# Diagonal matrices of inverse softmax sums in place of the identity, in the second and third attention of a three-layer block on one core

## The chip, the cores and the metric

The kernel runs on one core of a Trainium2 chip. The time is the device time of one execution in microseconds; the kernel before was timed in three runs, with a median of 2087.43 us and values from 2087.04 to 2091.03 us.

## The reference, cut to what matters

The program computes a stack of three blocks over 512 positions of width 1024, all in float32: a differential attention, a windowed attention with grouped keys and sinks, and a forgetting attention, each with projections and gated feed-forward parts around it. The change touches only how the softmax of the second and of the third attention is divided by its sum:

```python
# windowed attention (16 query heads, 4 key heads, blocks of 128 positions)
m = jnp.maximum(jnp.max(s, axis=-1, keepdims=True), sink)
e = jnp.exp(s - m)
pr = e / (jnp.sum(e, axis=-1, keepdims=True) + jnp.exp(sink - m))
o = jnp.einsum('bnhgqc,bnchd->bnqhgd', pr.astype(v.dtype), vb)
...
# forgetting attention (8 heads, causal, blocks of 128 queries)
p = jax.nn.softmax(s, axis=-1).astype(vh.dtype)
return jnp.einsum("bhqk,bhkd->bhqd", p, vh)
```

## The kernel before, in words

Activations are kept with the channels on the 128 partitions and the 512 positions along the row. Every large product is split: each float32 operand is written as a high and a low part in a rounded format (tiles with `hi` and `lo` in their names), and `mm3` (L546) issues three matrix products, high by high, high by low and low by high. Weights come in slabs of 128 x 1024 by DMA into `raw`; ScalarE rounds them to `whi` (L1090), GpSimd subtracts to get `wlo` (L536).

The three attentions are run by three functions of the same name, `attention(kind)`, one on TensorE, one on VectorE and one on ScalarE, each with kind 1, 2 or 3. The order is written by hand: a loop over steps `g`, four steps (one for each block of 128 queries) per pair of heads. Kind 2 has 8 pairs, so 32 steps, kind 3 has 4 pairs, so 16 steps. A step handles two heads `s`, and for its query block `nb` blocks of 128 keys: 2, 3, 3, 2 in kind 2 (the window), 1, 2, 3, 4 in kind 3 (causal). That makes 160 blocks of 128 x 128 in kind 2 and 80 in kind 3.

In step `g` each engine does, in this order:

- TensorE: `scores(g + 2)` (kind 2) or `scores(g + 1)` (kind 3); a quarter of a projection of later queries or keys as long as there are any (`piece`; in kind 2 for g up to 23, after the transposes where g is a multiple of 4), in kind 3 also parts of a gate's product from step 12 on; then `transposes(g)`, and in every second step `outputs(g - 1)`, the product with the values.
- VectorE: `maxima` of the scores just made, rotation of new queries and keys (`rope`, `q_low` L1743) or, in kind 3, their norm and some taps of a convolution (L2147), `normalise(g + 1)`, then `prob_low(g)`.
- ScalarE: the exponentials (L1207), which also give their sums, `prob_high(g)` (L1228, the transposed probabilities rounded from PSUM to `pthi`), and its share of the rest.

`normalise` adds the sink's term to the sums (kind 2, L1782), inverts the sums of both heads (L1793), and multiplies the probabilities of each head, `nb` x 128 columns, in place by the inverse sum of their row (L1797). `transposes` waits for that, and for `prob_low` of the step before, because a head's transposed probabilities stand in one of two PSUM banks (2 and 3) until `prob_low` (L1805) has read them. It then issues one transpose by TensorE for each block (L773), with the probabilities as the loaded operand and the identity as the one that streams through. The probabilities stand in the large buffer `AR`, the identity in `constR`. Elsewhere the kernel also has plain products of two float32 operands: `spread_norm` multiplies a column that is broadcast to 128 by the identity (tile `mixc` or `rcol` by `constR`), and `norm_sum` loads 128 x 128 blocks of `acc` and streams one column of ones. Both issue four products for one norm.

Of the kernel before, what the change touches and what calls it, by code (L numbers as in the profile page):

```python
# [29 lines left out]
ALU = mybir.AluOpType  # L30
# [6 lines left out]
P = 128  # L37
# [130 lines left out]
def slab_of(stage, i, j):  # L168

    s = SLAB0[stage] + j  # L170
    return s + 4 * i, s % RING, s // RAWS + (4 // RAWS) * i
# [15 lines left out]
def build(nc, xT, pT, posd, wts, par, con, lamd, outT):  # L187
    ctx = ExitStack()
    with ctx:
        def sb(name, shape, dt=F32):  # L190
            return ctx.enter_context(nc.sbuf_tensor(name, shape, dt))

        def sem(name):
            return ctx.enter_context(nc.semaphore(name))
# [15 lines left out]
        cosT = sb("cosT", [P, T])  # L210
# [16 lines left out]
        rinv = sb("rinv", [P, 8])  # L227
# [9 lines left out]
        PS = ctx.enter_context(nc.psum_tensor("PS", [P, 8, T], F32))  # L237
# [4 lines left out]
        def ar(off, n=1):  # L242
            v = AR[:, off:off + n * T]
            return v.rearrange("p (n t) -> p n t", n=n)
# [10 lines left out]
        def ccon(name, a=0, b=None):  # L255
            o, e = CCOLS[name]
            return con_sb[:, o + a:(e if b is None else o + b)]

        def f32(a):
            return a.bitcast(F32)  # L260
# [4 lines left out]
        ident = f32(identR)  # L265
# [7 lines left out]
            return ar(0, KC)[:, (m + 2) % KC, :]  # L273

        rC, rS = ar(0)[:, 0, :], ar(512)[:, 0, :]
        swap, qraw = ar(1024, 2), ar(2048, 2)
        prob = ar(3072, 4)
        OA = ar(5120, 8)
# [6 lines left out]
        def join_gate_of(m):  # L285
# [27 lines left out]
        score_done, max_ready, exp_ready, prob_ready = (  # L313
            sem("score_done"), sem("max_ready"), sem("exp_ready"), sem("prob_ready"))
# [60 lines left out]
        def band(kind, qb):  # L375


            if kind == 1:
                return 0, TB, []
            if kind == 2:  # L380
                lo, hi = max(qb - 1, 0), min(qb + 1, TB - 1)
                masks = [(qb - 1 - lo, 1)] * (qb > 0) + [(qb + 1 - lo, 2)] * (qb < TB - 1)
                return lo, hi - lo + 1, masks
            return 0, qb + 1, [(qb, 2)]
# [71 lines left out]
        def probs(kind):  # L456
            return prob3 if kind == 3 else prob
# [84 lines left out]
        def _(pe):  # L542
# [3 lines left out]
            def mm3(out, ahi, alo, bhi, blo, start, stop):  # L546
                mm(out, ahi, bhi, start, False)
                mm(out, ahi, blo, False, False)
                return mm(out, alo, bhi, False, stop)
# [5 lines left out]
            def open_tile(stage, i, j):  # L555
                bank, before = tile_of(stage, i, j)

                pe.wait_ge(tile_free[bank], before + 1)
                return PS[:, bank, :]
# [141 lines left out]
            def all_values(kind):  # L701

                stage = f"v{kind}"
                for t in range(4, 8) if kind == 1 else range(4):
                    bank, before = tile_of(stage, 0, t)
                    pe.wait_ge(tile_free[bank], before + 2)
# [54 lines left out]
            def transposes(kind, g):  # L761
                nb = band(kind, g % 4)[1]
                if g == 0 and kind == 1:
                    all_values(1)
                for s in range(HP[kind]):
                    n = PB0[kind] + HP[kind] * g + s

                    pe.wait_ge(prob_ready, n + 1)
                    if n >= 2:
                        pe.wait_ge(pt_ready, n - 1)  # L770
                    source = probs(kind)[:, 2 * (g % 2) + (1 if kind == 1 else s), :]
                    for k in range(nb):
                        last = pe.transpose(PS[:, 2 + n % 2, k * P:k * P + P],  # L773
                                            source[:, k * P:k * P + P], ident)
                    last.then_inc(trans_done, 1)

            def outputs(kind, g):
# [76 lines left out]
            def attention(kind, norm, begin):  # L854
# [10 lines left out]
                for g in range(steps):  # L865
# [13 lines left out]
                    if kind == 3:  # L879
                        for m, part in GATES.get(g, ()):  # L880
                            gate_part(m, part)
                    transposes(kind, g)
                    if kind == 3 and g == steps - 1:
                        for part in (2, 3):
# [122 lines left out]
            for k in range(KC):  # L1007
                last = mm3(PS[0:8, 6, :], wfhi[:, 8 * k:8 * k + 8], wflo[:, 8 * k:8 * k + 8],
                           hi[:, k, :], lo[:, k, :], k == 0, k == KC - 1)
# [45 lines left out]
            for q in range(4):  # L1055
                s, slot, _ = slab_of("ao3", 0, q)
                two_tiles("ao3", s, slot, 2 * q, lambda k: pthi[:, k, :], lambda k: ptlo[:, k, :])
            for what, n in JOIN:
                s, slot, _ = slab_of("gc3", 0, JOIN_SLAB[what, n])
                first = JOIN_TILE[what, n]  # L1060
                if what == "gate":
                    weights(s)
                    out = open_tile("gc3", 0, first)
                    for k in range(KC):
                        c = slice(k * P, k * P + P)
                        last = mm3(out, whi[:, slot, c], wlo[:, slot, c], hi[:, k, :], lo[:, k, :],
                                   k == 0, k == KC - 1)
# [535 lines left out]
        def _(dve):  # L1603
            own = Own(dve, dve_step)
            tt, stt, ts = dve.tensor_tensor, dve.scalar_tensor_tensor, dve.tensor_scalar
# [165 lines left out]
            def normalise(kind, g):  # L1771


                n = SC0[kind] + 2 * g
                nb = band(kind, g % 4)[1]
                pr, c, b = probs(kind), n % 4, 2 * (g % 2)

                dve.wait_ge(exp_ready, n + 2)
                if kind == 2:

                    dve.wait_ge(sink_ready, g + 1)
                    own.step(tt(rsum[:, c:c + 2], rsum[:, c:c + 2], rsum[:, 4 + c:6 + c], ALU.add))  # L1782
                    own.wait()
                if kind == 1:
                    own.step(dve.reciprocal(rinv[:, c + 1:c + 2], rsum[:, c + 1:c + 2]))
                    own.wait()
                    own.step(stt(rinv[:, c:c + 1], sum1[:, g:g + 1], lam[:, 5:6], rinv[:, c + 1:c + 2],
                                 ALU.mult, ALU.mult))
                    own.wait()
                    stt(pr[:, b + 1, :], pr[:, b + 1, :], rinv[:, c:c + 1], pr[:, b, :],  # L1790
                        ALU.mult, ALU.add).then_inc(prob_ready, 1)
                else:
                    own.step(dve.reciprocal(rinv[:, c:c + 2], rsum[:, c:c + 2]))  # L1793
                    own.wait()
                    for s in range(2):
                        v = pr[:, b + s, 0:nb * P]
                        ts(v, v, rinv[:, c + s:c + s + 1], None, ALU.mult).then_inc(prob_ready, 1)  # L1797

            def prob_low(kind, g):
                blocks = band(kind, g % 4)[1]  # L1800
# [46 lines left out]
            def attention(kind):  # L1847
# [3 lines left out]
                if kind == 3:  # L1851
                    maxima(kind, 0)
                    head_norm(2)
                    normalise(kind, 0)
                for g in range(steps):
# [16 lines left out]
                    if g + 1 < steps:  # L1872
                        normalise(kind, g + 1)
# [180 lines left out]
            for t in range(2):  # L2054
                q_low(t, 0, t)
            maxima(1, 0)
            normalise(1, 0)
            values_low("v1", (1,), T)
            rope_sin(0)
# [41 lines left out]
            for m in range(KC):  # L2101
                c = KC * NORMS.index("mix") + m
# [364 lines left out]
```

## Time and profile before

| | value |
|---|---|
| time, median of 3 runs | 2087.43 us |
| span of the profiled execution | 2087.8 us |
| TensorE busy | 2043.2 us (98%) |
| VectorE busy | 1224.2 us (59%) |
| ScalarE busy | 941.6 us (45%) |
| GpSimd busy | 904.8 us (43%) |
| mean granted TensorE clock | 0.992 |

The profile gives of the profiled execution's own time only its span, from the first to the last instruction; it stands 0.4 us above the median of the timed runs and inside their spread. A TensorE record's duration holds the time that the result needs to leave the engine, so records overlap, and the cost of one in a stream is the distance from its start to the next one's start. PE is TensorE, PEld its loads of the stationary operand, DVE is VectorE, ACT ScalarE, POOL GpSimd. A granted clock of 1.00 is 2.4 GHz, one of 0.50 is 1.2 GHz.

In the program's time the second attention lies at about 745 to 893 us, the third at about 1440 to 1547 us.

### The profile page before, as it was taken

Reading aid. Unit: us, or ns where it says so; the run is one execution under the profiler, and the core shown is the slowest. Engines: PE = TensorE matmul, PEld = TensorE weight load, DVE = VectorE, ACT = ScalarE, POOL = GpSimd, SP = SyncE. Lnnn points to the kernel's source line nnn. Section 1 sums busy time; section 2 is a strip of 40 time slices with the busy share of each in tenths; the row PEclk is TensorE's granted clock in tenths of the full one; section 3 lists DMA queues with packets and bytes.
Section 4 is the critical chain, followed back from the end, with each engine's and each line's share of the span. In section 5 each row is a group of like instructions: output and inputs, shape, how many; then the busy total and the mean of one; then the engine's idle time right before and its main releaser. Section 6 shows DMA issues by size and latency. Waiting matters only on the chain.

```text
span 2087.8 us, 28730 instructions
## 1 busy us (share of the span) xinstructions
PE 2043.2 (98%) x9976; PEld 1684.1 (81%) x9976; DVE 1224.2 (59%) x1842; ACT 941.6 (45%) x1495; POOL 904.8 (43%) x660
## 2 busy tenths in 40 slices
PE   7999999999999999899999999999999999999999
PEld 6777788888887878788888887878888788888887
DVE  6677857546265789856636266548879473213222
ACT  5456645434245567635424245535742544322222
POOL 4322235545456431044645456444215454455454
PEclk9999999999999999999999999999999999999999
DMA  4222122332323211022333223222103222232323
GB/s 169 81 76 76 48 75 98 103 101 91 101 91 121 81 61 32 31 91 81 101 101 101 92 99 112 91 81 92 39 23 107 85 91 92 90 110 92 101 91 111
DMA packets 52756, 183.21 MB, mean 88 GB/s; under 512 B 6576, under 2 KB 6832, under 8 KB 52656
## 3 DMA queue, kind: packets, MB, share of 16 engines
q1 hardware_dynamic: 51072, 177.76, 25.9%
q10 hardware_dynamic: 1584, 4.07, 0.5%
q8 instruction: 68, 1.11, 0.2%
q14 instruction: 32, 0.26, 0.0%
HBM read 176.04 MB, written 2.10 MB: 85 GB/s over the span
## 4 chain that ended last, share of the span: by engine, by line
PE 53%; issue 24%; POOL 13%; DVE 7%; ACT 2%; POOLq 0%; DVEq 0%; DMA 0%; ACTq 0%; SPq 0%
PE PS L544 52%; POOL wlo L536 13%; DVE AR L1915 1%; PE PS L773 1%; DVE AR L1918 0%; DVE acc L1630 0%; DVE ptlo L1805 0%; DVE AR L1797 0%; DVE nmax L1753 0%; ACT AR L1187 0%; DVE AR L2277 0%; ACT AR L1323 0%; DVE AR L1931 0%; DVE Blo L1935 0%; DVE Blo L2281 0%
## 5 line engine op out<-in xcount | busy, mean ns | idle before, releaser
L536 POOL TENSOR_TENSOR wlo<-raw,whi 128x512 fp32r<-128x512 f32 x656 | 904.6, 1402 | 1169.7 <-ACT whi L1090 1168.5
L544 PE MATMUL PS<-Bhi,whi 128*128 128x512 f32 x2352 | 927.7, 394 | 17.2 <-DVE Blo L1623 10.8
L544 PE MATMUL PS<-Blo,whi 128*128 128x512 f32 x2352 | 917.6, 390 | 0.0
L544 PE MATMUL PS<-Bhi,wlo 128*128 128x512 f32 x2352 | 917.4, 390 | 0.0
L1090 ACT ACTIVATE whi<-raw 128x1024 fp32r<-128x1024 f32 x328 | 345.2, 1056 | 510.7 <-PE PS L544 435.4
L544 PEld LDWEIGHTS PS<-Bhi,whi 128*128 128x128 f32 x2352 | 442.5, 188 | 123.1 <-issue 14.1
L544 PEld LDWEIGHTS PS<-Bhi,wlo 128*128 128x128 f32 x2352 | 442.6, 188 | 93.7
L544 PEld LDWEIGHTS PS<-Blo,whi 128*128 128x128 f32 x2352 | 443.0, 188 | 89.3 <-issue 0.5
L1614 DVE TENSOR_TENSOR AR<-PS,R 128x512 f32<-128x512 f32 x170 | 115.3, 690 | 235.9 <-PE PS L544 224.1
L1670 DVE TENSOR_TENSOR X<-X,PS 128x512 f32<-128x512 f32 x88 | 60.3, 687 | 227.2 <-PE PS L544 226.5
L1915 DVE SCALAR_TENSOR_TENSOR AR<-AR,par_sb 128x511 f32<-128x511 f32 x88 | 117.6, 1336 | 8.8 <-ACT AR L1323 8.8
L1338 ACT ACTIVATE Bhi<-AR 128x512 f32 x66 | 41.8, 633 | 167.7 <-DVE AR L1931 167.7
L1918 DVE SCALAR_TENSOR_TENSOR AR<-AR,par_sb 128x511 f32<-128x511 f32 x88 | 106.8, 1213 | 12.9 <-DVE AR L1915 2.9
L1207 ACT ACTIVATE AR<-PS,nmax 128x512 f32<-128x512 f32 (+3 forms) x160 | 93.2, 590 | 44.1 <-DVE nmax L1756 41.7
L1323 ACT ACTIVATE AR<-AR,par_sb 128x512 f32<-128x512 f32 x88 | 71.0, 806 | 38.5 <-DVE AR L1614 38.5
L1935 DVE TENSOR_TENSOR Blo<-AR,Bhi 128x512 f32 x66 | 47.1, 714 | 62.1 <-ACT Bhi L1338 62.1
L1623 DVE SCALAR_TENSOR_TENSOR Blo<-X,par_sb,Bhi 128x512 fp32r<-128x512 f32 x56 | 63.0, 1135 | 34.9 <-ACT Bhi L1116 27.7
L1228 ACT ACTIVATE pthi<-PS 128x512 fp32r<-128x512 f32 (+3 forms) x128 | 56.4, 477 | 59.1 <-PE PS L773 58.4
L1931 DVE TENSOR_TENSOR AR<-AR 128x512 f32<-128x512 f32 x66 | 56.1, 849 | 36.3 <-ACT AR L1334 27.2
L1630 DVE TENSOR_TENSOR acc<-acc,sq 128x512 f32<-128x512 f32 x56 | 73.2, 1308 | 0.0
L773 PE MATMUL PS<-constR,AR 128*128 128x128 f32 x368 | 58.3, 286 | 10.6 <-DVE ptlo L1805 9.7
L1805 DVE TENSOR_TENSOR ptlo<-PS,pthi 128x512 fp32r<-128x512 f32 (+3 forms) x128 | 64.3, 534 | 6.7 <-ACT pthi L1228 6.7
(237 smaller groups left out, 2069.1 us busy)
## 6 DMA issues: line engine op xcount, KB each, us to landing
raw<-in_weights SPq DMA_DIRECT2D x328, 512.0 KB, 3.2
AR<-AR SPq DMA_DIRECT2D x56, 64.0 KB, 2.0
X<-in_xT ACTq DMA_DIRECT2D x4, 512.0 KB, 6.9
out<-X SPq DMA_DIRECT2D x8, 256.0 KB, 3.0
AR<-in_pT ACTq DMA_DIRECT2D x2, 512.0 KB, 3.9
par_sb<-in_parameters ACTq DMA_DIRECT2D x1, 314.0 KB, 8.5
AR<-in_positions ACTq DMA_DIRECT2D x1, 256.0 KB, 8.3
con_sb<-in_constants ACTq DMA_DIRECT2D x1, 198.5 KB, 8.1
```

Source lines behind the costliest of these rows:

```text
L536: ins = pool.tensor_tensor(wlo[:, j, c], raw[:, j % RAWS, c], f32(whi[:, j, c]), ALU.subtract)
L544: return pe.matmul(out, w, x, start=start, stop=stop)
L773: last = pe.transpose(PS[:, 2 + n % 2, k * P:k * P + P], source[:, k * P:k * P + P], ident)
L1090: act.activation(whi[:, slot, :], raw[:, slot % RAWS, :], ACT.Copy)\
L1207: act.activation(probs(kind)[:, 2 * (g % 2) + s, 0:nb * P], PS[:, score_bank(kind, n), 0:nb * P], ACT.Exp, bias=nmax[:, n % 4:n % 4 + 1], ...
L1323: act.activation(cv[:, 2 * pair + u, :], us[:, 2 * pair + u, :], ACT.Identity, scale=conv_w[:, l, 1, u, bass.ds(q, 1)], bias=conv_w[:, l, ...
L1614: tt(out, PS[:, bank, :], R[:, :], ALU.mult).then_inc(tile_free[bank], 1)
L1623: stt(chunks(Blo[b])[:, m, :], X[:, m, :], gain(name, col, m), f32(chunks(Bhi[b])[:, m, :]), ALU.mult, ALU.subtract).then_inc(x_split, 1)
L1630: tt(acc[:, :], acc[:, :], sq[:, slot, :], ALU.add).then_inc(sq_used, 1)
L1805: tt(transposed(ptlo, kind, g, s), PS[:, 2 + n % 2, 0:blocks * P] .rearrange("p (k q) -> p k q", k=blocks), f32(transposed(pthi, kind, g, s)),
L1915: own.step(stt(c[:, 1:T], x[:, 0:T - 1], conv_w[:, l, 0, u, bass.ds(q, 1)], c[:, 1:T], ALU.mult, ALU.add))
L1918: stt(c[:, 0:T - 1], x[:, 1:T], conv_w[:, l, 2, u, bass.ds(q, 1)], c[:, 0:T - 1], ALU.mult, ALU.add).then_inc(conv_done, 1)
```

## The change

VectorE no longer multiplies the probabilities. For each head it multiplies the identity (the float32 copy in `con_sb`) by the inverse sums, which gives a 128 x 128 diagonal matrix, whatever `nb` is. There are four such matrices, in the columns of `cosT`, a tile of 512 columns that nothing else uses in these stretches. TensorE then multiplies each block of probabilities by the diagonal matrix of its head where it transposed it by the identity before: the result is the transposed block with its columns scaled. In place of the transpose instruction this is the plain product `mm` of two float32 operands. The first attention (kind 1) keeps the transpose. On every engine the instructions stand in the same order as before: 47 groups of transposes on TensorE and 48 pairs of multiplications on VectorE are exchanged in place (48 steps; at the end of the second attention the transposes of two steps adjoin and count as one group), and no wait or increment is added or moved.

```diff
+        diag = cosT[:, :].rearrange("p (n c) -> p n c", n=4)
...
                     for k in range(nb):
-                        last = pe.transpose(PS[:, 2 + n % 2, k * P:k * P + P],
-                                            source[:, k * P:k * P + P], ident)
+                        out, c = PS[:, 2 + n % 2, k * P:k * P + P], slice(k * P, k * P + P)
+                        if kind == 1:
+                            last = pe.transpose(out, source[:, c], ident)
+                        else:
+
+                            last = mm(out, source[:, c], diag[:, 2 * (g % 2) + s, :], True, True)
                     last.then_inc(trans_done, 1)
...
                     own.step(dve.reciprocal(rinv[:, c:c + 2], rsum[:, c:c + 2]))
                     own.wait()
                     for s in range(2):
-                        v = pr[:, b + s, 0:nb * P]
-                        ts(v, v, rinv[:, c + s:c + s + 1], None, ALU.mult).then_inc(prob_ready, 1)
+
+                        ts(diag[:, b + s, :], ccon("ident"), rinv[:, c + s:c + s + 1], None, ALU.mult)\
+                            .then_inc(prob_ready, 1)
```

## Rows read from the trace of the kernel before

**Rows 1.** The page: busy time by engine; then TensorE's busy share in 40 slices.

```profile
PE 2043.2 (98%) x9976; PEld 1684.1 (81%) x9976; DVE 1224.2 (59%) x1842; ACT 941.6 (45%) x1495; POOL 904.8 (43%) x660
...
PE   7999999999999999899999999999999999999999
```

**Rows 2.** Windows of both attentions: stretch, its length, busy time (and records) by engine.

```profile
757.00:857.00 100.00, 98.14 (x704) 81.73 (x705) 91.57 (x265) 71.16 (x209) 17.75 (x14) 0.98 0.12 38
857.00:886.00 29.00, 21.25 (x159) 18.37 (x158) 25.79 (x77) 21.86 (x64) 2.51 (x2) 0.88 0.06 19
1459.00:1505.00 46.00, 45.51 (x348) 38.41 (x347) 37.95 (x82) 31.74 (x65) 8.07 (x6) 1.00 0.11 36
1505.00:1531.00 26.00, 21.23 (x157) 18.61 (x158) 24.15 (x53) 15.60 (x38) 2.98 (x2) 0.80 0.06 22
1531.00:1548.00 17.00, 17.00 (x116) 14.73 (x115) 11.87 (x25) 6.85 (x18) 0.00 (x0) 1.00 0.00 0
```

**Rows 3.** Line 773: all its transposes; then those of the stretch 757 to 857 us.

```profile
L773 PE MATMUL PS<-constR,AR x368: 270/272/476, 89.9 to 1546.4; 128*128 128x128 f32 x184
...
757.00:857.00 100.00, 17.85 (x120) 13.99 (x120) 0.98 0.12 38
```

**Rows 4.** Timeline of TensorE, transposes in the second attention: start us, duration us, operation.

```profile
788.47 0.60 PE L773 MATMUL PS<-constR,AR 128*128 128x128 f32 x4
...
789.96 0.74 PE L773 MATMUL PS<-constR,AR 128*128 128x128 f32 x4
...
796.59 0.82 PE L773 MATMUL PS<-constR,AR 128*128 128x128 f32 x6
797.51 0.39 PE L544 MATMUL PS<-qkhi 64*128 64x256 f32 x2
```

**Rows 5.** Timeline: four products in `spread_norm`; weight loads of four in `norm_sum`.

```profile
1382.98 1.05 PE L544 MATMUL PS<-constR,mixc 128*128 128x128 f32 x8
1383.79 0.48 PE L544 MATMUL PS<-Bhi,whi 128*128 128x512 f32 x1
...
681.60 1.08 PEld L544 LDWEIGHTS PS<-con_sb,acc 128*128 128x128 f32 x8
```

**Rows 6.** Groups of VectorE instructions, shapes apart, line 1797: busy us, mean ns of one.

```profile
L1797 DVE TENSOR_SCALAR AR<-AR,rinv 128x384 f32<-128x384 f32 x40 | 15.0, 418 | 0.7
...
L1797 DVE TENSOR_SCALAR AR<-AR,rinv 128x256 f32<-128x256 f32 x40 | 14.0, 392 | 0.7
...
L1797 DVE TENSOR_SCALAR AR<-AR,rinv 128x512 f32<-128x512 f32 x8 | 3.5, 484 | 0.1
...
L1797 DVE TENSOR_SCALAR AR<-AR,rinv 128x128 f32<-128x128 f32 x8 | 1.9, 283 | 0.1
```

**Rows 7.** Waits at 757 to 857 us, then 857 to 886 us: us, times, longest.

```profile
PE PS L544 <- DVE AR L1716: 2.4, 1, 2.4
...
PE PS L773 <- DVE ptlo L1805: 5.9, 5, 2.2
...
PE PS L544 <- DVE ptlo L1805: 1.4, 1, 1.4
```

**Rows 8.** Timeline of one step late in the second attention.

```profile
870.45 0.66 PE L773 MATMUL PS<-constR,AR 128*128 128x128 f32 x4
870.55 1.02 DVE L1753 TENSOR_REDUCE nmax<-PS 128x1 f32<-128x384 f32 x2 [1.12 <-PE PS L544]
...
872.88 0.75 DVE L1805 TENSOR_TENSOR ptlo<-PS,pthi 128x256 fp32r<-128x256 f32 x2
...
873.45 0.74 PE L773 MATMUL PS<-constR,AR 128*128 128x128 f32 x4 [1.38 <-DVE ptlo L1805]
```

**Rows 9.** Windows with the granted clock at half (third number from the end).

```profile
758.80:762.20 3.40, 3.40 (x17) 2.40 (x16) 3.29 (x10) 3.11 (x9) 1.22 (x1) 0.51 0.00 0
861.20:868.10 6.90, 5.59 (x30) 5.06 (x30) 6.48 (x21) 6.02 (x19) 2.51 (x2) 0.51 0.01 2
1520.00:1530.20 10.20, 9.25 (x49) 7.94 (x48) 9.57 (x24) 5.12 (x16) 0.00 (x0) 0.50 0.01 2
```

## The prediction

> **What bounds the kernel now.** I read the page first. TensorE is busy for 98% of the span, no other engine for more than 59%, and of the 40 slices only the first and one in the middle are below 9 tenths [rows 1]. So TensorE's own stream sets the time nearly everywhere, and time added to it is added to the kernel, except where it stands idle anyway. That makes the windows over the two attentions the second view [rows 2]. From 757 to 857 us (steps 1 to 24 of the second attention) TensorE is busy for 98.14 of 100 us. In the last steps, 857 to 886 us, no projection is left to fill its stream: 21.25 of 29 us, with VectorE at 25.79. The third attention is full up to 1505 us (45.51 of 46) and after 1531 us (17.00 of 17); between, where steps 8 to 11 have neither projection nor gate, TensorE has 21.23 of 26 and VectorE 24.15. The waits give the idle time its name: in the stretch at 857 us, 5.9 + 1.4 us are for `ptlo` of VectorE, and in the full stretch 2.4 us is one single wait for VectorE's L1716, right at the start [rows 7].
>
> **Removed: the transposes.** Kinds 2 and 3 hold 160 + 80 = 240 of the 368 transposes (the other 128 are the first attention's, unchanged), and 368 blocks leave 368 records: one record for a block [rows 3]. Six of them last 0.82 us from the first start to the last end [rows 4], the last one 0.27 us [rows 3], so they start (0.82 - 0.27) / 5 = 0.110 us apart.
>
> **Added: the float32 products.** No row shows this very product, but `spread_norm` has its twin: 128 x 128 float32 loaded, 128 float32 columns streamed. Its four products leave eight records, over 1.05 us [rows 5]; less the last one's 0.27 that is 0.78 / 7 = 0.111 us from record to record, and two records for a product: 0.223 us. A broadcast operand isn't the reason for the doubling, since four dense blocks of `acc` in `norm_sum` also take eight loads [rows 5]. So a block goes from 0.110 to 0.223 us: 0.113 us more, and 240 blocks are 27.1 us if nothing hides any of it. That is the upper end; the lower is 0, if a block's product came in one record like a transpose.
>
> The Trainium skill ("FP8 and Floating Point Precision", TensorE Precision Notes) says that a true float32 product takes four passes, and "TensorE: Matmul & The Clock Gate" (Terms) that the transpose mode is four times faster for float32. By these a block would cost four times 0.110 us rather than two. The trace has two records where the page has four passes, and it agrees in direction but not in size; the sum goes by the trace, and the page's ratio is a rival below.
>
> **Changed: VectorE's multiplication.** The 96 instructions of L1797 now take 15.0 + 14.0 + 3.5 + 1.9 = 34.4 us; each becomes one of 128 columns, and the nearest row, the same form at 128 columns, has 283 ns, so 96 x 0.283 = 27.2 us [rows 6]. VectorE gets 7.2 us back: 0.27 us for a step with three blocks to a head, 0.22 with two, 0.40 with four, nothing with one. The other end is nothing saved. Where TensorE is the bound this is worth 0, because its work hides it.
>
> **What of it is on the path.**
>
> Step 0 of the second attention (4 blocks) stands before the wait of 2.4 us for L1716 [rows 7]: 0.45 us is hidden there. If this cover is gone it costs just that.
>
> Steps 1 to 24 hold 120 blocks [rows 3], all in the full stream: 120 x 0.113 = 13.6 us. Against it stand small waits that longer products cover. After a burst of six transposes the scores start 0.92 us after its first start [rows 4], though 5 x 0.110 + 0.20 (the same distance after an undisturbed burst, an estimate) would be 0.75; with 0.68 us more work ahead this 0.17 us goes, six times: 1.0 us. And every fourth step has two bursts 1.5 us apart, of which the second takes 0.74 us against 0.60 for the first [rows 4], since its banks are still being read; the longer first burst covers that: 6 x 0.14 = 0.8 us. What is left is 13.6 - 1.8 = 11.8 us.
>
> Steps 25 to 31 hold 36 blocks, 4.1 us. Of two consecutive steps, the one without `outputs` is VectorE's: after the scores at 870.4 it works without a break through maxima, inverse, multiplication and `ptlo` up to 873.6, while TensorE waits 1.38 us for it [rows 8]. There the longer product (0.45 to 0.68 us) is hidden, and VectorE's 0.22 to 0.27 us come through. In the other step TensorE runs through transposes, `outputs` and scores and waits hardly at all, so the product counts in full. I take half of each: +2.0 us, and half of VectorE's 1.7 us back, -0.8: +1.2 us. The ends are -1.7 (all hidden) and +4.1.
>
> Third attention: 80 blocks. Steps 0 to 7 and 12 to 15 are in full stretches [rows 2] and step 11 is followed by full work: 68 blocks. Of the 12 of steps 8 to 10 I count 2 as exposed, the rest stands beside VectorE's chain. 70 x 0.113 = 7.9 us; VectorE's gain in steps 9 to 11, 0.22 + 0.27 + 0.40 = 0.9 us, shortens that chain: +7.0 us. The ends are +6 and +9.
>
> The clock: inside the attentions TensorE was granted half its clock for 3.4, 6.9 and 10.2 us, the second and third of these in and behind the stretches with idle time [rows 9, 2]. Half speed costs at most half of each, 10.2 us together, less where TensorE waits anyway. The change fills some of that idle time, which speaks for shorter half-clock stretches, but the stretches also shift; I take -1.0 us, with -9 and +4 as ends.
>
> **The sum.** 11.8 + 1.2 + 7.0 - 1.0 = 19.0 us. The profiled span of 2087.8 us becomes 2106.8; since it lies 0.4 us above the median of the runs, I predict 2106.5 us, 0.9% slower.
>
> **The rivals.**
> - *The half clock goes.* If the idle time that goes takes all three half-clock stretches with it, up to 9 us come back instead of 1: 2098.5 us. For it: the two longest stand where TensorE idles most. Against: the one at 758.8 us follows a wait that stays, and half the tail's idle stays. 9%.
> - *Everything exposed, and new waits behind it.* `pthi` and with it `ptlo` come up to 0.68 us later in a step; if VectorE and ScalarE have no slack for that, the tail's steps grow too: 27.1 us and some for further waits, about 2117 us. Against: VectorE reaches `ptlo` long after `pthi` is there [rows 8]. 7%.
> - *VectorE is the bound (the other side).* If `ptlo`, not TensorE's stream, set the pace of all steps of both attentions, the products would run in idle time and the 7.2 us of VectorE would be the result: 2080.5 us. It decides from the point where TensorE's idle time in these stretches exceeds the 27.1 us added; the five stretches have 1.86 + 7.75 + 0.49 + 4.77 + 0 = 14.9 us [rows 2], half of it in two short ones. 2%.
> - *No doubling.* If a dense block by a diagonal matrix left one record like a transpose, only VectorE's gain in the short stretches would count: about 2086 us. Both rows of float32 products speak against it. 2%.
> - *Four times.* If a block went to 4 x 0.110 us, 0.33 us more, 240 blocks would add 79 us, less some 8 hidden: about 2159 us. Against it the same rows. 1%.
>
> **How the numbers follow.** The forecast has 79%, between 2100 and 2114 us. The range for 8 times in 10 reaches a little into the two nearest rivals: 2099 to 2115 us. A measurement of this kernel can tell about 0.2% (4 us) from no change. Faster by more than that: the VectorE rival and a sliver of others, 0.03. Within it: no doubling, 0.02. Slower: 0.95.
>
> **What the profile after should show.** 480 records for 240 blocks, at 0.11 us from start to start, under line 546 with `cosT` and `AR`; 128 transposes left. The 96 multiplications at about 283 ns each. The stretch of steps 1 to 24 some 12 us longer with TensorE still full; the late steps' waits for `ptlo` shorter; the rest of the program unchanged to within a microsecond or two. One record for a block, or records at another distance, would break the main term; an attention that grows by less than 15 us together with full half-clock stretches would mean that more is hidden than I took.

## The result and the profile after

The changed kernel takes 2101.41 us (median of six runs, 2099.98 to 2105.55) against 2087.31 for the kernel before in the same comparison: 14.1 us more, ratio 1.0068 with a 95% interval from 1.0057 to 1.0079. Forecast were 2106.5 us and +19.0 us. On another chip, measured again beside the experiments, the ratio was 1.0068 (1.0055 to 1.0082).

The profiled span went from 2087.8 to 2099.7 us. The page after, first busy times, then TensorE's busy share in 40 slices, as in [rows 1]:

```profile
PE 2061.4 (98%) x10216; PEld 1709.3 (81%) x10216; DVE 1223.0 (58%) x1842; ACT 945.3 (45%) x1495; POOL 903.2 (43%) x660
...
PE   7999999999999999999999999999999999999999
```

TensorE has 240 records more and 18.2 us more busy time; every other engine is within 4 us of before. The one slice in the middle that was below 9 tenths, over the late steps of the second attention, shows a 9 now.

The products, by tile, and VectorE's part, as groups (busy us, mean ns of one, idle time before), as in [rows 3, 6]:

```profile
L546 PE MATMUL PS<-cosT,AR x480: 270/275/551, 752.1 to 1558.3; 128*128 128x128 f32 x160
```

```profile
L1803 DVE TENSOR_SCALAR cosT<-con_sb,rinv 128x128 f32<-128x128 f32 x96 | 24.8, 301 | 1.7
```

480 records for 240 blocks: two for each, where a transpose left one. The 96 multiplications keep VectorE busy for 24.8 us where L1797 took 34.4; I had put them at 27.2. One of them lasts 301 ns, a little more than the 283 I took; the busy time is less than 96 times that because instructions overlap in it.

Timeline of TensorE, the same places as in [rows 4], start and duration in us:

```profile
788.31 1.05 PE L546 MATMUL PS<-cosT,AR 128*128 128x128 f32 x8
...
797.06 1.50 PE L546 MATMUL PS<-cosT,AR 128*128 128x128 f32 x12
798.49 0.39 PE L546 MATMUL PS<-qkhi 64*128 64x256 f32 x2
```

Twelve records of six blocks last 1.50 us; less the last one's 0.27 that is 1.23 / 11 = 0.112 us each, so 0.224 us a block. The forecast had 0.223. The scores start 1.43 us after the burst does; it was 0.92.

The windows at the places of [rows 2], shifted with the program:

```profile
760.20:864.60 104.40, 104.40 (x801) 92.71 (x800) 88.80 (x251) 68.27 (x195) 15.39 (x13) 1.00 0.11 36
864.60:893.00 28.40, 23.25 (x204) 21.56 (x203) 25.32 (x78) 21.79 (x64) 2.52 (x2) 1.00 0.07 20
1465.00:1514.00 49.00, 49.00 (x375) 42.48 (x375) 37.51 (x84) 32.82 (x66) 8.07 (x6) 1.00 0.11 39
1514.00:1541.00 27.00, 22.89 (x196) 20.84 (x193) 22.39 (x50) 15.81 (x38) 2.98 (x2) 0.94 0.06 20
```

In the late steps TensorE still idles, but its granted clock, the third number from the end, is 1.00 there instead of 0.88. In steps 8 to 11 of the third attention it is 0.94 instead of 0.80.

To see where the time went, the start of the same burst of blocks is read from each kernel's timeline, and the program cut at five places: A from step 0 to step 25 of the second attention, B from there to step 0 of the third, C to its step 8, D to its step 12, E to the end. The last two columns are the us at half clock inside B and D; a piece at half clock that begins up to 0.5 us before B is counted whole. Each row comes from one profiled execution. The rows of the experiments are used below.

| kernel | A | B | C | D | E | half B | half D |
|---|---|---|---|---|---|---|---|
| before | 106.7 | 597.7 | 47.6 | 24.8 | 556.0 | 6.8 | 10.2 |
| changed | 116.9 | 596.9 | 51.4 | 24.2 | 558.2 | 0 | 3.4 |
| changed, again | 117.0 | 597.0 | 51.4 | 22.9 | 558.2 | 0 | 3.4 |
| product by the identity | 117.4 | 597.7 | 51.4 | 24.9 | 558.2 | 0 | 3.4 |
| diagonal not used | 106.9 | 598.9 | 47.1 | 22.9 | 555.9 | 10.2 | 6.8 |
| product twice | 141.4 | 603.3 | 60.3 | 24.7 | 562.7 | 0 | 0 |
| rounded product, kind 2 | 105.3 | 605.0 | 51.4 | 22.7 | 558.2 | 27.3 | 0 |
| second attention alone | 117.0 | 596.7 | 47.5 | 24.9 | 555.9 | 0 | 10.2 |
| third attention alone | 106.7 | 597.5 | 51.4 | 22.9 | 558.2 | 6.8 | 3.4 |
| product in late steps only | 106.4 | 596.9 | 47.5 | 24.1 | 556.0 | 0 | 3.4 |
| late transposes twice | 106.7 | 597.7 | 47.5 | 25.0 | 555.9 | 3.4 | 10.2 |
| product in full steps only | 116.6 | 600.0 | 51.4 | 24.7 | 558.2 | 10.2 | 10.2 |
| rounded in full steps | 105.2 | 597.2 | 47.5 | 24.2 | 556.0 | 3.4 | 3.4 |

From step 0 on the changed kernel is 10.2 - 0.8 + 3.8 - 0.5 + 2.2 = 14.9 us longer, within a microsecond of the medians' 14.1. The two spans differ by only 11.9 because the changed kernel reached step 0 at 752.1 us and the profile of before at 755.1. That isn't the change's: the same changed kernel, profiled again, reached it at 755.2 us, and the kernel with the change in the second attention alone, whose code up to there is the same, at 755.7 us. The first attention waits for the small transfers of `exchange`, and these waits differ between executions:

```profile
DVE AR L1743 <- DMA AR<-AR: 5.6, 9, 1.2
```

```profile
DVE AR L1743 <- DMA AR<-AR: 9.9, 10, 2.1
```

The first is the wait in the changed kernel from 85 to 265 us (us, times, longest), the second the same in the kernel with the second attention alone.

### The profile page after: what moved, and what is told of

The parts are those of the page before. It is cut to its first block, busy times and chain, and to the rows that moved or that the text cites. A ratio compares the mean times of both kernels' runs of the same rounds, so it can differ in the third digit from the quotient of the medians.

```text
span 2099.7 us, 29210 instructions
## 1 busy us (share of the span) xinstructions
PE 2061.4 (98%) x10216; PEld 1709.3 (81%) x10216; DVE 1223.0 (58%) x1842; ACT 945.3 (45%) x1495; POOL 903.2 (43%) x660
## 4 chain that ended last, share of the span: by engine, by line
PE 55%; issue 23%; POOL 13%; DVE 6%; ACT 1%; POOLq 0%; DVEq 0%; DMA 0%; ACTq 0%; SPq 0%
PE PS L546 55%; POOL wlo L538 13%; DVE AR L1922 1%; DVE AR L1925 0%; DVE acc L1636 0%; DVE AR L2284 0%; ACT AR L1329 0%; DVE AR L1938 0%; DVE Blo L1942 0%; DVE Blo L2288 0%; ACT Bhi L1122 0%; DVE AR L1620 0%; ACT whi L1096 0%; ACT Bhi L1344 0%; DVE X L1676 0%
## 5 line engine op out<-in xcount | busy, mean ns | idle before, releaser
L546 PEld LDWEIGHTS PS<-Bhi,whi 128*128 128x128 f32 x2352 | 442.2, 188 | 120.9 <-issue 11.6
L1676 DVE TENSOR_TENSOR X<-X,PS 128x512 f32<-128x512 f32 x88 | 60.3, 687 | 227.1 <-PE PS L546 226.4
L1942 DVE TENSOR_TENSOR Blo<-AR,Bhi 128x512 f32 x66 | 47.1, 714 | 62.1 <-ACT Bhi L1344 62.1
L1938 DVE TENSOR_TENSOR AR<-AR 128x512 f32<-128x512 f32 x66 | 56.1, 849 | 36.3 <-ACT AR L1340 27.2
L1812 DVE TENSOR_TENSOR ptlo<-PS,pthi 128x512 fp32r<-128x512 f32 (+3 forms) x128 | 65.9, 535 | 13.7 <-ACT pthi L1234 12.9
L546 PE MATMUL PS<-cosT,AR 128*128 128x128 f32 x480 | 65.2, 284 | 7.0 <-DVE ptlo L1812 7.0
```

What stands on the lines that cost most here:

```text
L546: return pe.matmul(out, w, x, start=start, stop=stop)
L1676: tt(X[:, m, :], X[:, m, :], PS[:, bank, :], ALU.add)\
L1812: tt(transposed(ptlo, kind, g, s), PS[:, 2 + n % 2, 0:blocks * P] .rearrange("p (k q) -> p k q", k=blocks), f32(transposed(pthi, kind, g, s)),
```

## The experiments

Each ratio is to the kernel before on the same chip, with its 95% interval.

**Product by the identity.** VectorE scales the probabilities as before, TensorE multiplies by the identity.

```diff
-                        last = pe.transpose(PS[:, 2 + n % 2, k * P:k * P + P],
-                                            source[:, k * P:k * P + P], ident)
+                        out, c = PS[:, 2 + n % 2, k * P:k * P + P], slice(k * P, k * P + P)
+                        if kind == 1:
+                            last = pe.transpose(out, source[:, c], ident)
+                        else:
+                            last = mm(out, source[:, c], ident, True, True)
```

> The kernel before, with the transposes of the second and third attention as float32 products by the identity; VectorE scales the probabilities as before. Theory A (the doubling of the records is the whole cost, VectorE's shorter multiplication is worth only a little where VectorE sets the pace): 2102 to 2104 us, 0.5 to 2.5 us above the changed kernel's 2101.4; steps 1 to 24 of the second attention some 11 us longer than before, as in the changed kernel. Theory B (the products cost nearly their full 27 us and VectorE's 7 us were what brought it down to 14): 2108 us or more. Half-clock stretches: if the fuller stream of products is what shortened them, they are short here too (mean clock 0.996); if they shift by chance, anything from 0.992 to 0.997.

Measured: 2103.90 us, ratio 1.0074 (1.0060 to 1.0088). The whole cost of the change is there without the diagonal matrices. Its profile is 2.0 us longer than the changed kernel's; burst by burst it falls behind by 0.2 us in steps 1 to 24, 1.1 us in the late steps and 0.7 us in stretch D, so VectorE's shorter work is worth 2 us and not 7. That rests on one profile of each; the ratios of the timed runs, 1.0074 and 1.0068, overlap in their intervals. Theory A holds.

**Diagonal not used.** VectorE as changed, TensorE as before.

```diff
-                            last = mm(out, source[:, c], diag[:, 2 * (g % 2) + s, :], True, True)
+                            last = pe.transpose(out, source[:, c], ident)
```

> The changed kernel's VectorE work (diagonal matrices instead of scaled probabilities) with the old transposes by the identity; the division by the sums is thereby left out of the second and third attention. Theory A: only the short stretches in which VectorE sets the pace gain, 1 to 2.5 us: 2085 to 2086.5 us, and the half clock late in the second attention stays. Theory B: most of VectorE's 7.2 us show: 2080 to 2082 us.

Measured: 2086.43 us, 2.5 us below its before, ratio 0.9989 (0.9980 to 0.9998). From the other side about the same 2 us. The late steps kept their half clock (10.2 us of it) and stretch B is 1.2 us longer than before, although VectorE has less to do: what it saves there is taken by the clock. The two pieces of B that are longer than before, step 26 and the part from step 31 on, are pieces with time at half clock.

**Product twice.**

```diff
+                            mm(out, source[:, c], diag[:, 2 * (g % 2) + s, :], True, True)
                             last = mm(out, source[:, c], diag[:, 2 * (g % 2) + s, :], True, True)
```

> The changed kernel with each product by a diagonal matrix issued twice into the same place (four records for a block). Theory A (0.111 us a record, and the small waits were already covered by the first doubling, so the second is exposed in full in steps 1 to 24 and 3/4 of it elsewhere): 120 x 0.223 = 26.8 us in steps 1 to 24, about 20 us in the rest: 2146 to 2150 us. Theory C (the stretches have slack that a product of any length goes on using, as half of the first doubling did): 120 x 0.223 / 2 and the like, 2125 to 2130 us.

Measured: 2148.90 us, ratio 1.0290 (1.0274 to 1.0306), as theory A had it. Six blocks in the timeline are now 24 records:

```profile
807.25 2.84 PE L546 MATMUL PS<-cosT,AR 128*128 128x128 f32 x24
```

(2.84 - 0.27) / 23 = 0.112 us a record. Step 8 to step 24 of the second attention, 80 blocks, take 66.25 us before, 73.46 changed, 91.34 here. The second doubling costs 17.88 us, 0.2235 a block, in full; the first cost 7.21 us, where 80 x 0.113 is 9.04. So in these 16 steps 1.8 us of small waits were covered by the first doubling and none was left for the second. In stretch C it is 8.9 us for 40 blocks, again 0.223 each. The Trainium skill ("FP8 and Floating Point Precision", TensorE Precision Notes) gives a float32 product four passes; the trace has two records of 0.112 us for it and four only when it is issued twice, so the estimate of twice a transpose was right for this burst of 128 columns. It doesn't speak against four passes as such. With 512 columns, in the kernel before, four float32 products leave eight records too:

```profile
L544 PE MATMUL PS<-AR,con_sb x8: 591/592/592, 1617.4 to 1620.4; 128*128 128x512 f32 x8
```

(1620.4 - 1617.4) / 7 = 0.43 us a record, 0.86 us a product, where the rounded products of 512 columns just before start 0.23 us apart. There a float32 product costs close to four rounded ones.

**Rounded product in the second attention.**

```diff
+        prob2 = Bhi[1][:, 2048:4096].rearrange("p (n t) -> p n t", n=4)
+        diag2 = Blo[1][:, 2048:2560].rearrange("p (n c) -> p n c", n=4)
...
-            return prob3 if kind == 3 else prob
+            return {1: prob, 2: prob2, 3: prob3}[kind]
```

> The changed kernel, but in the second attention the exponentials and the diagonal matrices are written in the rounded format (in halves of the value buffers that are free there), so that the product is one of rounded operands; the low part of these probabilities is lost. Third attention as changed. Theory A (a record of rounded operands with 128 columns takes 0.06 us, as the value product's 128-column records do at best, and there is one for a block): steps 1 to 24 are 120 x (0.223 - 0.06) = 19.6 us shorter than changed, less some 2 us of waits that come back; total 2084 to 2088 us. Theory D (the load of 128 columns sets the distance, 0.11 us): 120 x 0.11 = 13.5 us shorter, less the same waits: 2090 to 2093 us.

Measured: 2097.74 us, ratio 1.0040 (1.0025 to 1.0055), outside both expectations. Six blocks are six records:

```profile
794.32 0.78 PE L548 MATMUL PS<-Blo,Bhi 128*128 128x128 f32 x6
```

With a last record of 0.28 us that is 0.50 / 5 = 0.10 us a block: one record instead of two, and nearly as long as a transpose, not 0.06. On the record theory A is wrong and D right, and stretch A did shrink by 11.6 us, to 1.4 us below before, as D had it (13.5 less some 2). The gain was lost in the late steps (36 us from step 25 on; third number from the end the clock):

```profile
858.40:894.40 36.00, 31.20 (x160) 28.85 (x161) 23.05 (x69) 18.54 (x55) 2.51 (x2) 0.62 0.05 16
```

The clock was at half for 27.3 us of stretch B, which is 8.1 us longer than in the changed kernel. All of that lies in the pieces with time at half clock: step 26 takes 7.08 us instead of 4.57, step 28 5.10 instead of 3.89, step 30 5.26 instead of 3.52, the part from step 31 on 2.6 us more; the steps between them are as long as in the changed kernel to 0.01 us. For the load of 128 columns "TensorE: Matmul & The Clock Gate" of the Trainium skill (LDWEIGHTS) gives columns / 1.2 in ns, by which an estimate for 128 columns is 107 ns; the distances of 0.10 to 0.112 us of all three kinds of record agree with a stream of such small products being paced by their loads, though no run separates load and stream.

**One attention alone.** The condition on `kind` is the edit.

```diff
-                        if kind == 1:
+                        if kind != 2:
                             last = pe.transpose(out, source[:, c], ident)
```

> The change made in the second attention alone; the third keeps its transposes and scaled probabilities. Theory A (each attention pays for its own blocks: about 10 us in steps 0 to 24, near nothing or a gain in the late steps, where the products stand beside VectorE's work and the half clock goes): the stretch from step 0 to the third attention grows by 9 to 10 us, as in the changed kernel, and the time is 2096 to 2099 us. By the terms of the prediction it would be 11.8 + 1.2 us, 2100 to 2101 us.

Measured: 2095.89 us, ratio 1.0033 (1.0021 to 1.0044), 7.0 us above its before and just below the expected 2096 to 2099. A + B are 9.3 us longer in the profile, which is of the slowest of its seven executions.

> The change made in the third attention alone. Theory A: its 80 blocks cost 5 to 7 us, 2092.5 to 2094.5 us, and the half clock late in the second attention (6.9 us in the profile of before) is there again, since that attention has its idle time back. Theory C (the stretches of half clock come by chance and not with TensorE's idle time): it may be missing there.

Measured (`if kind != 3`): 2095.18 us, ratio 1.0030 (1.0019 to 1.0041), 6.3 us: inside the expected 5 to 7 us, though just above the 2092.5 to 2094.5 us, since this chip's before is 2088.9. The two add to 13.3 us, the change's 14.1 within the intervals. The late steps of the second attention, with their transposes back, had half clock again, 6.8 us.

**Product in the late steps only.**

```diff
+        def by_product(kind, g):
+            return (kind == 2 and g > 24) or (kind == 3 and 8 <= g <= 11)
...
-                        if kind == 1:
+                        if not by_product(kind, g):
...
+                        v = pr[:, b + s, 0:nb * P]
+                        out, src = (diag[:, b + s, :], ccon("ident")) if by_product(kind, g) else (v, v)
+                        ts(out, src, rinv[:, c + s:c + s + 1], None, ALU.mult).then_inc(prob_ready, 1)
```

> Diagonal matrices and products only in the steps without a projection to fill TensorE's stream (25 to 31 of the second attention, 8 to 11 of the third), transposes and scaled probabilities in all others. Theory A (there the products run in TensorE's idle time, VectorE's shorter work comes through, and the half clock goes): 1 to 3 us below before, 2085 to 2087 us by the chip's before of about 2088, and steps 1 to 24 as before. Theory B (the products cost there too): 36 + 20 blocks x 0.113 = 6.3 us above before.

Measured: 2087.00 us, 1.9 us below its before, ratio 0.9988 (0.9979 to 0.9997). The 6.3 us of TensorE's work added in these steps cost little. Against the kernel with the same VectorE work and transposes (diagonal not used) step 28 is 0.4 us longer (3.88 and 3.50), step 9 of the third attention 0.2 us (4.34 and 4.18) and its step 11, which full work follows, 1.1 us (7.23 and 6.13, with 3.4 and 3.0 us at half clock). In D the half clock didn't go wholly: 3.4 us are left. The same 36 us from step 25 on, first here, then with the same VectorE work but transposes (diagonal not used):

```profile
859.20:895.20 36.00, 32.05 (x231) 28.76 (x232) 23.20 (x70) 18.98 (x56) 2.50 (x2) 1.00 0.05 16
```

```profile
859.90:895.90 36.00, 30.45 (x186) 26.50 (x187) 22.88 (x69) 18.67 (x55) 2.52 (x2) 0.86 0.05 16
```

Clock 1.00 against 0.86, and a stretch B of 596.9 against 598.9 us: the kernel that does more is through it sooner. The difference stands in step 26 (4.56 against 5.53 us) and from step 31 on (576.0 against 577.4 us), both with 3.4 to 3.6 us at half clock in the kernel with transposes.

**Late transposes twice.**

```diff
-                        last = pe.transpose(PS[:, 2 + n % 2, k * P:k * P + P],
-                                            source[:, k * P:k * P + P], ident)
+                        for _ in range(2 if (kind == 2 and g > 24) else 1):
+                            last = pe.transpose(PS[:, 2 + n % 2, k * P:k * P + P],
+                                                source[:, k * P:k * P + P], ident)
```

> The kernel before with each transpose of steps 25 to 31 of the second attention issued twice, 36 more records of 0.11 us (4.0 us of TensorE work), VectorE's work as before. Theory A (the work goes into TensorE's idle time, and with it the granted clock stays full there): the stretch from step 25 to the projections after it is as long as before or up to 1.5 us shorter, no half clock in it, time within 0.1% of before. Theory C (the clock has nothing to do with it): the stretch is about 2 us longer and has its half clock as before.

Measured: 2088.08 us, ratio 0.9994 (0.9985 to 1.0003). 4.0 us more work, stretch B as long as before to 0.1 us, half clock down from 6.8 to 3.4 us but not gone. Theory C's 2 us are not there; theory A's "no half clock" isn't either. The mean clock of its 11 timed executions is 0.9935, between the 0.9923 of this chip's before and the 0.9955 of the product in the late steps.

```profile
860.10:896.10 36.00, 32.16 (x226) 28.54 (x227) 24.87 (x69) 18.55 (x55) 2.53 (x2) 0.95 0.05 16
```

**Product in the full steps only.** The condition of `by_product` is turned round.

```diff
+            return (kind == 2 and g <= 24) or (kind == 3 and not 8 <= g <= 11)
```

> The complement of the kernel with products in the late steps only: diagonal matrices and products in steps 0 to 24 of the second attention and 0 to 7 and 12 to 15 of the third, transposes and scaled probabilities elsewhere. Theory A (the blocks of the full steps carry the whole cost, the late ones give some back): 10.2 us in steps 0 to 24 as in the changed kernel, 6.0 us in the third attention, about 2105 us, 1 to 3 us above the changed kernel on the same chip. Theory B (late steps cost too): below the changed kernel.

Measured: 2107.09 us, ratio 1.0090 (1.0075 to 1.0105), 4.4 us above the changed kernel on the same chip, with fewer products and more than the 1 to 3 us expected. The late steps here are word for word those of before, yet stretch B is 600.0 us instead of 597.7, with 10.2 us at half clock instead of 6.8 (B and D together are 4.8 us longer here than in the changed kernel again, A 0.4 us shorter):

```profile
871.40:907.40 36.00, 30.00 (x186) 26.63 (x187) 23.67 (x69) 18.04 (x55) 2.71 (x2) 0.86 0.05 16
```

**The changed kernel again.**

> The changed kernel itself, beside the others on the same chip: 2101 to 2104 us, so that the single kernels can be compared with it without the difference between chips.

Measured: 2102.68 us, ratio 1.0068 (1.0055 to 1.0082).

**Rounded product in the full steps, float32 product in the late ones.** In the second attention up to step 24 as in the rounded kernel, in the third transposes outside steps 8 to 11. The diagonal matrices are chosen by step in the same way (left out of the cut).

```diff
+            return kind == 2 or (kind == 3 and 8 <= g <= 11)
...
+            return {1: prob, 2: prob if g > 24 else prob2, 3: prob3}[kind]
```

> Second attention: in steps 0 to 24 exponentials and diagonal matrices in the rounded format and one rounded product for a block (0.10 us), in steps 25 to 31 the float32 product; third attention: the float32 product in steps 8 to 11, transposes in the rest. The probabilities of those 25 steps lose their low part. By the stretches measured apart: steps 0 to 24 1.4 us shorter than before, the late steps 0.8 us shorter, the third attention 0.8 us shorter: about 3 us below before, 2085 to 2086.5 us. If the half clock comes back in the late steps as in the kernel with rounded products throughout the second attention, it is 3 to 6 us more.

Measured: 2084.29 us, 4.0 us below its before, ratio 0.9981 (0.9971 to 0.9991): the shortest of all, and 0.7 us below the expected 2085 to 2086.5. Stretch A is 1.5 us, B 0.4 us, D 0.6 us shorter than before. It isn't the same result at a lower price: the probabilities of 25 steps lose their low part.

## Why the prediction was right in direction and a third too high

**Right: the doubling, and where it is paid.** Two records of 0.112 us for a block instead of one of 0.110 was the term that carries the sum, and both the profile after and the doubled product confirm it. In full steps without waits it is exact: stretch E has 20 blocks and grew by 2.2 us, 20 x 0.113 = 2.3.

**Right: VectorE's saving hardly counts.** I had 1.7 us for it (0.8 and 0.9); identity against diagonal shows 2.0 us: 0.5 in A, which I had at nothing, 0.8 in B and 0.7 in D. The 7.2 us that I gave as VectorE's whole saving set busy time, in which overlapping instructions count once, against 96 times a mean. Busy time against busy time it is 34.4 - 24.8 = 9.6 us. The sum didn't use it; it used the means by step.

**Too small: the waits that longer products cover.** For steps 1 to 24 I took 1.8 us off 13.6; stretch A, with step 0, grew by 10.2 us. Step 0 cost nothing, as forecast (8.27 us before, 8.23 after, from its burst to the next one's). Read so step by step, four steps repeat through the stretch; here are steps 8 to 11, in us:

| step | blocks | before | changed | grown | by count |
|---|---|---|---|---|---|
| 8 | 4 | 6.63 | 6.80 | 0.17 | 0.45 |
| 9 | 6 | 3.13 | 3.63 | 0.50 | 0.68 |
| 10 | 6 | 5.29 | 5.99 | 0.70 | 0.68 |
| 11 | 4 | 1.50 | 1.94 | 0.44 | 0.45 |

Steps 10 and 11 pay in full. In steps like 9 the 0.17 us before the scores are covered, six times, 1.1 us together, as forecast. The term that was too small is that of steps like 8: 0.28 us each instead of 0.14. Of the 0.14 us by which "takes 0.74 us against 0.60" only 0.04 went: the burst's eight records now start over 0.88 us, where undisturbed ones would over 7 x 0.111 = 0.78. What I overlooked there is TensorE's short stop before the late projection, where the distance to the next product went from 0.31 to 0.12 us. And step 24 doesn't belong to the full stretch: there VectorE's shorter work for step 25 comes through, and the step went from 5.58 to 5.26 us (5.52 with the identity, where VectorE's work is as before), so its 4 blocks, 0.45 us, were hidden. The idle time of the weight loads shows the stops, at 757 to 857 us before and 760 to 864 after:

```profile
PEld PS L544 <- issue: 7.0, 18, 2.6
PEld PS L544 <- DVE qklo L1743: 2.0, 6, 0.4
```

```profile
PEld PS L546 <- issue: 1.8, 5, 0.4
```

The two windows aren't quite the same place: 3.2 of the 7.0 us, the longest of 2.6 among them, stand before step 1. From step 1 on it is 3.8 + 2.0 us before and 1.8 after. In stretch C, of 4.5 us by count 3.8 showed: 0.4 us was hidden in step 1, which held a wait of 0.4 us for VectorE's L2214, and 0.2 in step 7, since the burst after it no longer stops 0.22 us for `ptlo`.

**Mis-sized: the late steps and the clock.** I had +1.2 us for steps 25 to 31 and -1.0 us for the clock in both attentions together. Stretch B was 0.8 us shorter, D 0.5 us shorter where my terms gave about +0.2. A step without `outputs` does hide the product, as told. The step of [rows 8], after (the view ends inside the last burst, so it counts 5 of its 8 records):

```profile
876.86 1.16 PE L546 MATMUL PS<-cosT,AR 128*128 128x128 f32 x8
876.96 1.02 DVE L1759 TENSOR_REDUCE nmax<-PS 128x1 f32<-128x384 f32 x2 [0.39 <-PE PS L546]
...
879.17 0.75 DVE L1812 TENSOR_TENSOR ptlo<-PS,pthi 128x256 fp32r<-128x256 f32 x2
879.73 0.79 PE L546 MATMUL PS<-cosT,AR 128*128 128x128 f32 x5 [0.74 <-DVE ptlo L1812]
```

From burst to burst it is 2.87 us instead of 3.00, and the wait fell from 1.38 to 0.74 us. What was wrong is the other half, the steps with `outputs`, where I counted the product in full, 2.0 us. The kernel before and the product by the identity differ in the product alone and are both at full clock in steps 27 to 30: 3.00, 3.50, 3.04 and 3.66 us against 2.99, 3.89, 3.04 and 3.66. Only step 28 pays, 0.4 us; step 25 is as long as before too, and step 26 can't be compared so, since before has half clock in it. VectorE's 0.8 us came in as forecast. So the product's 1.6 us too much, more than the clock's 0.5 us, is what was off in B.

The clock was worth some more than the 1 us I gave it, and how much depends on where the half clock lies. Where VectorE sets the pace it costs nothing: step 25 takes 3.58 us with 3.6 us at half clock (before) and at full clock (identity), step 10 of the third attention 5.54 us with 4.4 at half and 5.53 at full. Where TensorE has full work it costs near half of its length: step 11 takes 7.19 us with 3.3 at half in the changed kernel and 5.66 at full in the same kernel profiled again, which had its 3.4 us in step 10 and is 1.3 us shorter in D for it. In B step 26 went from 5.08 us (2.7 at half) to 4.57, 0.5 us. In D two kernels with transposes in step 11 take 7.35 us with 5.8 at half (before) and 6.13 with 3.0 (diagonal not used); by that rate the 2.5 us that the changed kernel has less there are 1.1 us. My estimate from these is 1.6 us for the clock. The kernel with products in the full steps only is 2.3 us longer in B than before for 3.4 us more of half clock; 1.7 of it stand in steps 26 and 30, at half clock, and 0.6 from step 31 on, where neither kernel has any, so that part is not the clock's.

All six kernels with the float32 product throughout the late steps of B and nothing rounded (changed, again, by the identity, twice, second attention alone, late steps only) had no half clock in B; all five with transposes there had 3.4 to 10.2 us; the one with rounded products only up to step 24 had 3.4. In D all eight kernels with the product had 0 to 3.4 us and all five with transposes 6.8 to 10.2. The timed executions say the same: mean clock 0.995 to 0.997 in all 11 of the changed kernel, 0.990 to 0.995 in the 56 of before beside the experiments. Even so, the rival in which the half clock goes, at 2098.5 us, did not come true: 3.4 of 10.2 us stayed in D, 3.4 us near step 0 stayed, and some 1.6 us came back instead of up to 9. That the piece near step 0 stayed was partly luck: it is missing in three other profiles (diagonal not used, product twice, full steps only), though the last has the changed kernel's code up to step 24.

By stretches: 11.8 forecast and 10.2 measured in A, 1.2 and -0.8 in B, 7.0 and 5.5 in C to E, and -1.0 for the clock that the measured values already hold: 19.0 and 14.9 us. One reading of the prediction was wrong without harm to the sum: of the 14.9 us of idle time in the five stretches 7.75 + 4.77 = 12.5 us stand in the two short ones, not half.

**Open.** Whether the half clock goes because TensorE's stream is fuller isn't settled. Transposes doubled filled it by about as much as the products do (32.16 and 32.05 us busy in the 36 from step 25 on) and left 3.4 us; rounded products, with about the stream of transposes, had 27.3 us. That could be the kind of instruction or the moment at which the stretch begins; telling these apart needs the same stream started at different times, which wasn't tried. Chance has a part in it: before step 0 of the second attention all 13 profiled executions run the same instructions, and they show 6.8 to 13.7 us at half clock there. Nor was it tried to change the DMA waits in the first attention that set apart single executions.

## What to carry to other kernels

Folding a scaling into a transpose by using a diagonal matrix isn't free where the operands are float32: the transpose leaves one record, the product two of the same length. Where TensorE's stream is full, count it in full, and take off the short stops between its groups too, those that no engine is named for: here 2.9 of 13.6 us (stretch A with the identity grew by 10.7). Where another engine sets the pace the product costs little, so such a change is best made step by step: in the steps without filler alone it gained 1.9 us, everywhere it cost 14.1. Even there the last step before full work, step 11 of the third attention, paid some 1.1 us; to leave it out wasn't tried.

## What the runs showed of the hardware that I had not expected

- A rounded product with 128 columns is no cheaper than a float32 transpose of the same block: 0.10 and 0.11 us, although it leaves one record too and the float32 product takes 0.224. With 512 columns it is 0.23 us for a rounded product and 0.86 for a float32 one.
- More TensorE work can shorten a stretch: with the same VectorE work, products in the late steps gave 596.9 us for stretch B at full clock, transposes 598.9 us with 10.2 us at half clock.
- The same 3.4 us at half clock cost 1.5 us in one execution of the changed kernel (step 11, full work) and 0.2 us in another (step 10, where VectorE sets the pace: 5.30 us against 5.13).
- A gain in front can be lost behind: rounded products saved 11.6 us in stretch A against the changed kernel, and 8.1 us of it were lost in stretch B to a clock at half for 27.3 us.
